# A one-core hybrid decoder step: the order of the down projection and of the rows going back in the later pairs' steps

## Chip, cores and metric

The kernel runs on one core of one Trainium2 chip. The metric is device time of one execution in microseconds (us), lower is better.

## What is computed

The reference is one inference step of two layers over 256 prompt tokens and 32 sample tokens (288 rows of 1024 values, float32). Each layer mixes the tokens (a recurrent group, a convolution group and a retention group) and then applies a mixture of 32 experts of which each token uses two. The change lies in the expert part:

```
def hier_moe(x, wg, bg, we, be, w1, w3, w2):
    ...
    def expert(acc, params):
        w1e, w3e, w2e, ge = params
        h = jax.nn.silu(xt @ w1e) * (xt @ w3e)
        return acc + ge[:, None] * (h @ w2e).astype(jnp.float32), None
```

w1 and w3 of an expert are 1024 x 256, w2 is 256 x 1024, each 1 MB in float32. The two layers hold 192 MB of them, and all of it is read in every execution.

## The kernel before

**Pairs and steps.** The experts are taken in 16 pairs per layer. An expert has 64 slots for tokens, so a pair fills 128 partitions. TensorE (PE) works through `experts2_back(p)`, one call per pair p from 4 to 15 (the first four pairs have a shorter form, `experts2`). In a step of pair p, TensorE issues in this order:

- `up` (L1149) of the pair's first expert: 16 matmuls with w1 and w3, "first up" below;
- `give_back(p - 2, (2, 3))` and `give_back(p - 2, (4,))` (L1195, L1201, L1186), where pair p - 2 is one of `BY_MATMUL`: a 0/1 matrix takes the weighted rows of that pair back to the tokens' places, in three bf16 parts that add up to the float32 value (`y_top`, `y_mid`, `y_low`). Parts 2 and 3 are the second 128 tokens, part 4 the 32 sample rows;
- `down` (L1172) of pair p - 1: the second projection, 8 matmuls with w2, into two PSUM banks (`y0`, `y1`);
- `turn_h` (L749): two transposes of the first expert's hidden values;
- `tokens` half 0 (L749), the second `up`, `tokens` half 1, the second `turn_h`;
- `give_back(p - 1, (0, 1))`: the first 128 tokens of pair p - 1.

`BY_MATMUL` is every pair but 0 to 3, 8 and 9, whose rows go by way of DRAM instead. So parts 2, 3 and 4 are given back in steps 6 to 9 and 12 to 15, in eight steps of a layer. Steps 4, 5, 10 and 11 go through the same function without them. Step 15 has no `tokens`, and its second `turn_h` comes after the function.

**Other engines.** ScalarE (`one_back`, L2235) copies the first hidden values out of PSUM (L2241), waits for part 4 of pair p - 2, whose parts still read the buffer `ysb`, and then writes the two halves of pair p - 1 there (`results`, L2214). Behind them in its order stands the tanh of the first expert (L2233). VectorE (`experts2_back`, L1962) adds parts 2 and 3 (L1950) and 4 (L1954) to `x`, then computes the rest of the first half (L1915), the first expert's hidden product (L1903, L1905), the rest of the second half (L1915), the two low parts (L1921), and takes the next pair's tokens out of PSUM (L1895). `give_back(p - 1, (0, 1))` waits for the low parts (L1199). In steps 13 to 15 VectorE also adds rows that were read back from DRAM (L1938).

**Weights.** SyncE issues all weight loads on one queue, in a fixed order (L669 to L693), into a ring of 12 places of 1 MB. In its step p it issues w1 and w3 of the first expert of p, then waits for `y1` of pair p - 3 and issues the w2 of pair p - 1 (L557, `expert2`), then w1 and w3 of the second expert. `up` and `down` wait for the landings (`granule`). GpSimd gathers the token rows and builds the 0/1 matrices (L2376).

Of the kernel before, what the change touches and what calls it, by code (L numbers as in the profile page):

```python
# [205 lines left out]
def build(nc, ins, outs):  # L206
# [11 lines left out]
    with ExitStack() as ctx:  # L218
# [151 lines left out]
        def weight13(e, j, k):  # L370

            if (e, j) == (THIRD, 0):
                return third_w1[k]
            if e == EARLY:
                k0, a = [pc for pc in (early_w1, early_w3)[j] if pc[0] <= k][-1]
                return a[:, FE * (k - k0):FE * (k - k0) + FE]
            if e == SPARE:
                return (spare_w1, spare_w3)[j][:, k, :]
            return ring[:, 3 * (e % 4) + j, FE * k:FE * k + FE]

        def weight2(e, f, j):

            if e == EARLY:
                f0, j0, a = [pc for pc in early_w2 if pc[0:2] <= (f, j)][-1]
                return a[:, 512 * (j - j0):512 * (j - j0) + 512]
            if e == SPARE:
                return spare_w2[f][:, 512 * j:512 * j + 512]
            return ring[:, 3 * (e % 4) + 2, 1024 * f + 512 * j:1024 * f + 512 * j + 512]
# [103 lines left out]
        def xfreed(eng, kind, u, it, l):  # L492
            b, n = expert_job(kind, u, it, l)
            eng.wait_ge(bank_free[b], n + 1)

        def pair_of(p):

            return p % 2, p // 2

        def granule(eng, l, g, use):  # L500

            spared = [e // 4 for e in (EARLY, SPARE, *((THIRD,) if g % 3 == 0 else ())) if e % 4 == g // 3]
            per = 1 + (g >= 8) + GROUPS - len(spared)
            k = {"in": 0, "out": 1}[use] if isinstance(use, str) else 1 + (g >= 8) + use[0] - sum(it < use[0] for it in spared)
            eng.wait_ge(granule_in[g], 16 * (l * per + k + 1))
# [231 lines left out]
        def _(pe):  # L737
# [10 lines left out]
            def transpose(out, in_, n):  # L748
                return pe.transpose(out, in_, ident[0:n, 0:n])  # L749
# [42 lines left out]
            for l in range(DEPTH):  # L792
# [319 lines left out]
                def begin(kind, u, it):  # L1112
                    b, n = expert_job(kind, u, it, l)
                    pe.wait_ge(bank_free[b], n)
                    return psum[:, b, :]

                def finish(i, kind, u, it=0):
                    i.then_inc(bank_full[expert_job(kind, u, it, l)[0]], 1)

                def tokens(g2, it, halves=(0, 1)):  # L1120

                    par = g2 % 2
                    if 0 in halves:
                        pe.wait_ge(gath[par], 16 * (l * GROUPS + it + g2 // 2 + 1))
                    for kind, k0 in [(("x0", 0), ("x1", 4))[h] for h in halves]:
                        b = begin(kind, g2, it).rearrange("p (k s) -> p k s", k=4)
                        r = rows[:, par, :].rearrange("p (m k) -> p m k", k=KT)
                        for k in range(4):
                            i = transpose(b[:, k, :], r[:, :, k0 + k], 128)
                        finish(i, kind, g2)  # L1130

                def up(u, it):

                    e = 4 * it + u
                    if e in (EARLY, SPARE, THIRD):
                        pe.wait_ge(spare13_in, 16 * 15 * (l + 1))
                    if e not in (EARLY, SPARE):
                        if e != THIRD:
                            granule(pe, l, 3 * u, (it,))
                        granule(pe, l, 3 * u + 1, (it,))  # L1140
                    if u % 2 == 0:
                        xfreed(pe, "x0", u // 2, it, l)
                    b = begin("h", u, it)
                    s = slice(SLOTS * (u % 2), SLOTS * (u % 2) + SLOTS)
                    for k in range(KT):
                        if (u % 2, k) == (0, 4):
                            xfreed(pe, "x1", u // 2, it, l)
                        for j in range(2):
                            i = pe.matmul(b[64 * j:64 * j + 64, 0:FE], xsT[:, u // 2, k, s], weight13(e, j, k), start=k == 0,  # L1149
                                          stop=k == KT - 1, skip_group_check=True)  # L1150
                    finish(i, "h", u)

                def turn_h(u, it):
                    xfreed(pe, "h", u, it, l)
                    b = begin("hT", u, it)
                    for f in range(2):
                        i = transpose(b[:, 128 * f:128 * f + 128], hsb[:, u % 2, 128 * f:128 * f + 128], 128)
                    finish(i, "hT", u)

                def down(pair, it):  # L1160

                    for u in (2 * pair, 2 * pair + 1):
                        if 4 * it + u in (EARLY, SPARE):
                            pe.wait_ge(spare2_in, 16 * 5 * (l + 1))
                        else:
                            granule(pe, l, 3 * u + 2, (it,))
                    xfreed(pe, "hT", 2 * pair + 1, it, l)
                    for j in range(2):
                        b = begin(f"y{j}", pair, it)
                        for f in range(2):  # L1170
                            for q in range(2):
                                i = pe.matmul(b[64 * q:64 * q + 64, :], hT[:, q, f, :], weight2(4 * it + 2 * pair + q, f, j), start=f == 0,  # L1172
                                              stop=f == 1, skip_group_check=True)
                        finish(i, f"y{j}", pair)

                def give_back(p, parts):

                    pair, it = pair_of(p)
                    turn_ = l * len(BY_MATMUL) + BY_MATMUL.index(p)
                    if 0 in parts:  # L1180
                        pe.wait_ge(back_ready, turn_ + 1)
                    if 4 in parts:
                        b = begin("back4", pair, it)
                        for n_, y in enumerate((y_top, y_mid, y_low)):
                            for q in range(4):
                                i = pe.matmul(b[32 * q:32 * q + 32, 0:256], back[:, pair, SEQ:NT], y[:, 256 * q:256 * q + 256],  # L1186
                                              start=n_ == 0, stop=n_ == 2, skip_group_check=True)
                        finish(i, "back4", pair, it)
                        return
                    banks = []  # L1190
                    for a in parts:
                        if a < 2:
                            xfreed(pe, f"y{a % 2}", pair, it, l)
                        banks.append(begin(f"back{a}", pair, it))
                        pe.matmul(banks[-1], back[:, pair, 64 * (a - a % 2):64 * (a - a % 2) + 128], y_top[:, 512 * (a % 2):512 * (a % 2) + 512],  # L1195
                                  start=True, stop=False)
                    for a, b in zip(parts, banks):
                        if a < 2:
                            pe.wait_ge(low_ready, 2 * (turn_ - l) + a + 1)  # L1199
                        for y in (y_mid, y_low):  # L1200
                            i = pe.matmul(b, back[:, pair, 64 * (a - a % 2):64 * (a - a % 2) + 128], y[:, 512 * (a % 2):512 * (a % 2) + 512],  # L1201
                                          start=False, stop=y is y_low)
                        finish(i, f"back{a}", pair, it)
# [25 lines left out]
                def experts2_back(p):  # L1229

                    pair, it = pair_of(p)
                    up(2 * pair, it)
                    if p - 2 in BY_MATMUL:
                        give_back(p - 2, (2, 3))
                        give_back(p - 2, (4,))
                    down(1 - pair, it if pair else it - 1)
                    turn_h(2 * pair, it)
                    if p + 1 < NPAIR:
                        tokens(pair + 1, it, (0,))
                    up(2 * pair + 1, it)  # L1240
                    if p + 1 < NPAIR:
                        tokens(pair + 1, it, (1,))
                        turn_h(2 * pair + 1, it)
                    if p - 1 in BY_MATMUL:
                        give_back(p - 1, (0, 1))
# [1203 lines left out]
```

## Time and profile before

| what | value |
|---|---|
| runs without a profile | 838.98, 837.44, 840.12 us, median 838.98 |
| the profiled execution's own time | 839.37 us |
| its span, first to last instruction | 837.5 us |
| TensorE busy with matmuls | 811.5 us, 97% |
| VectorE, ScalarE, GpSimd busy | 477.8, 176.0, 132.6 us |
| packets of SyncE's queue | 247.01 MB, 77.1% of 16 DMA engines' span |
| granted TensorE clock, mean | 0.996 |

The times are microseconds from the span's start. A row of the trace's timeline gives start, duration, engine, line and operation; rows of one kind that follow each other are merged. A float32 matmul is recorded twice (as two passes), so `x32` in such a row is 16 matmuls of the program. Each matmul's duration includes its passage through the array, so the time of a block is read from its start to the start of the next block. "Issue" as the cause of a wait means that the profile shows no instruction that released it; a landing of a load on which TensorE waited is of that kind here.

### The profile page before, as it was taken

Reading aid. Unit: us, or ns where it says so; the run is one execution under the profiler, and the core shown is the slowest. Engines: PE = TensorE matmul, PEld = TensorE weight load, DVE = VectorE, ACT = ScalarE, POOL = GpSimd, SP = SyncE. Lnnn points to the kernel's source line nnn. Section 1 sums busy time; section 2 is a strip of 40 time slices with the busy share of each in tenths; the row PEclk is TensorE's granted clock in tenths of the full one; section 3 lists DMA queues with packets and bytes.
Section 4 is the critical chain, followed back from the end, with each engine's and each line's share of the span. In section 5 each row is a group of like instructions: output and inputs, shape, how many; then the busy total and the mean of one; then the engine's idle time right before and its main releaser. Section 6 shows DMA issues by size and latency. Waiting matters only on the chain.

```text
span 837.5 us, 13390 instructions
## 1 busy us (share of the span) xinstructions
PE 811.5 (97%) x5250; PEld 459.4 (55%) x5250; DVE 477.8 (57%) x1101; ACT 176.0 (21%) x361; POOL 132.6 (16%) x201
## 2 busy tenths in 40 slices
PE   7999999999999999999999999999999999999995
PEld 4664554586555545455466545547755545555452
DVE  3497788264115554467655977764611455446676
ACT  3214122311221111211221221142022111121113
POOL 0031020011121202431000400200211311115120
PEclk9999999999999999999999999999999999999999
DMA  9942973879999999999990329348799999999971
GB/s 321 321 148 122 374 186 99 290 251 393 415 416 414 414 416 413 413 400 414 348 349 6 151 107 295 106 104 332 303 406 414 417 412 418 413 414 392 414 318 61
DMA packets 91962, 259.64 MB, mean 310 GB/s; under 512 B 30764, under 2 KB 42432, under 8 KB 76218
## 3 DMA queue, kind: packets, MB, share of 16 engines
q1 hardware_dynamic: 82426, 247.01, 77.1%
q0 software_dynamic: 7680, 8.91, 3.2%
q10 hardware_dynamic: 1792, 2.84, 0.9%
q8 instruction: 44, 0.72, 0.4%
q14 instruction: 20, 0.16, 0.1%
HBM read 265.22 MB, written 15.18 MB: 335 GB/s over the span
## 4 chain that ended last, share of the span: by engine, by line
PE 89%; DVE 5%; issue 2%; SPq 2%; ACT 1%; DMA 1%; DVEq 0%; ACTq 0%
PE psum L1149 28%; PE psum L1172 13%; PE psum L809 13%; PE psum L749 8%; PE psum L818 7%; PE psum L1006 4%; PE psum L1201 4%; PE psum L1195 2%; PE psum L828 2%; PE psum L755 1%; PE psum L1045 1%; DMA ring<-in_w_in 1%; PE psum L1186 1%; PE psum L884 1%; PE psum L1035 1%
## 5 line engine op out<-in xcount | busy, mean ns | idle before, releaser
L1149 PE MATMUL psum<-ring,arena 128*64 128x256 f32 x1888 | 220.5, 382 | 2.7 <-issue 1.2
L1149 PEld LDWEIGHTS psum<-ring,arena 128*64 128x64 f32 x1888 | 135.5, 137 | 70.5 <-issue 12.1
L1172 PE MATMUL psum<-ring,arena 128*64 128x512 f32 x480 | 116.2, 596 | 1.7 <-issue 1.7
L809 PE MATMUL psum<-ring,uT 128*128 128x512 f32 x256 | 113.6, 596 | 0.9 <-DVE uT L1383 0.9
L1950 DVE TENSOR_TENSOR x<-x,psum 128x512 f32<-128x512 f32 x80 | 51.4, 683 | 50.3 <-PE psum L1201 45.2
L1895 DVE TENSOR_TENSOR arena<-psum,gff 128x512 f32<-128x512 f32 x64 | 43.6, 686 | 61.0 <-PE psum L749 61.0
L809 PEld LDWEIGHTS psum<-ring,uT 128*128 128x128 f32 x256 | 47.6, 190 | 55.2 <-issue 54.2
L2353 POOL DMA_INDIRECT rows<-xn_scratch,sg x32 | 33.7, 1054 | 233.7 <-PE psum L749 118.1
L2214 ACT ACTIVATE arena<-psum,sg 128x512 f32<-128x512 f32 x64 | 44.0, 687 | 114.9 <-PE psum L1172 113.0
L1903 DVE SCALAR_TENSOR_TENSOR arena<-arena,psum 128x128 f32<-128x128 f32 x64 | 18.4, 287 | 85.7 <-ACT arena L2233 72.1
L1172 PEld LDWEIGHTS psum<-ring,arena 128*64 128x64 f32 x480 | 35.4, 137 | 54.6 <-issue 52.8
L818 PE MATMUL psum<-uT,ring 128*128 128x288 f32 x256 | 63.8, 407 | 0.7 <-DMA ring<-in_w_in 0.7
L1006 PE MATMUL psum<-ring,mixT 128*128 128x512 f32 x128 | 58.9, 612 | 0.0
L2241 ACT ACTIVATE arena<-psum 128x256 f32<-128x256 f32 x48 | 18.4, 383 | 186.1 <-PE psum L1149 186.1
L1470 DVE SCALAR_TENSOR_TENSOR cb<-glp,prm,cb 128x256 f32<-128x256 f32 x120 | 55.8, 534 | 0.6 <-DVE hst L1622 0.4
L818 PEld LDWEIGHTS psum<-uT,ring 128*128 128x128 f32 x256 | 48.1, 190 | 14.6 <-DMA ring<-in_w_in 1.1
L749 PE MATMUL psum<-const,rows 128*128 128x128 f32 (+1 forms) x304 | 47.9, 286 | 0.0
L749 PEld LDWEIGHTS psum<-const,rows 128*128 128x128 f32 (+1 forms) x304 | 39.1, 192 | 13.8 <-issue 12.8
L1915 DVE TENSOR_TENSOR v<-arena 128x512 f32<-128x512 f32 x36 | 24.8, 688 | 32.6 <-ACT arena L2214 32.6
L1006 PEld LDWEIGHTS psum<-ring,mixT 128*128 128x128 f32 x128 | 24.3, 195 | 28.1 <-issue 27.7
L2376 POOL TENSOR_SCALAR kT<-const,sg 128x128 bf16<-128x128 f32 (+3 forms) x60 | 36.7, 626 | 18.0 <-PE psum L1186 17.4
L1954 DVE TENSOR_TENSOR x<-x,psum 32x256 f32<-32x256 f32 x80 | 33.0, 413 | 0.8
(350 smaller groups left out, 908.9 us busy)
## 6 DMA issues: line engine op xcount, KB each, us to landing
ring<-in_moe_w SPq DMA_DIRECT2D x178, 1024.0 KB, 18.0
ring<-in_w_in SPq DMA_DIRECT2D x24, 1024.0 KB, 13.8
ring<-in_w_out SPq DMA_DIRECT2D x8, 1024.0 KB, 7.3
y_scratch<-in_w_out SPq DMA_DIRECT2D x1, 2304.0 KB, 17.8
arena<-in_state_ret SPq DMA_DIRECT2D x16, 128.0 KB, 5.9
out<-arena SPq DMA_DIRECT2D x16, 128.0 KB, 2.5
xn_scratch<-rows ACTq DMA_DIRECT2D x4, 512.0 KB, 4.5
mixT<-in_moe_w SPq DMA_DIRECT2D x2, 1024.0 KB, 4.9
```

The lines of the kernel that those rows point to most:

```text
L749: return pe.transpose(out, in_, ident[0:n, 0:n])
L809: i = pe.matmul(b, uTk[:, k, 128 * t:128 * t + 128], w[:, k, :], start=k == 0, stop=k == KT - 1)
L818: i = pe.matmul(b, w[:, k, 128 * (c % 4):128 * (c % 4) + 128], uTk[:, k, :], start=k == 0, stop=k == KT - 1)
L1006: i = pe.matmul(b, mixT[:, k, 128 * t:128 * t + 128], w[:, :, k, :], start=k == 0, stop=k == 3, skip_group_check=True)
L1149: i = pe.matmul(b[64 * j:64 * j + 64, 0:FE], xsT[:, u // 2, k, s], weight13(e, j, k), start=k == 0, stop=k == KT - 1, skip_group_check=True)
L1172: i = pe.matmul(b[64 * q:64 * q + 64, :], hT[:, q, f, :], weight2(4 * it + 2 * pair + q, f, j), start=f == 0, stop=f == 1, skip_group_chec ...
L1470: chain[c] = own(STT(dst, glp[:, c, k:k + SEQ], w, dst, ALU.mult, ALU.add))
L1895: T(xsT[:, g2 % 2, k0:k0 + 4, :], psum[:, b, :].rearrange("p (k s) -> p k s", k=4), g3[:, k0:k0 + 4, :], ALU.mult).then_inc(bank_free[b], 1)
L1950: i = T(s, s, psum[:, b, :], ALU.add)
L2214: A(ysb[:, 512 * j:512 * j + 512], psum[:, b, :], ACT.Copy, scale=gate_col[:, pair:pair + 1]).then_inc(bank_free[b], 1)
L2353: pool.indirect_dma_start(out=rows[:, g % 2, :], out_offset=None, in_=xn_dram, in_offset=bass.IndirectOffsetOnAxis(ap=gidx[:, g:g + 1], ax ...
L2376: i = pool.tensor_scalar(back[:, g % 2, o:o + n] if g < NPAIR - 1 else back_last[:, o:o + n], C("iota")[:, 0:n], tok[:, t, g:g + 1], None, ...
```

## The change

```diff
@@ -1230,11 +1230,11 @@ (experts2_back, on TensorE)
                     pair, it = pair_of(p)
                     up(2 * pair, it)
+                    down(1 - pair, it if pair else it - 1)
+                    turn_h(2 * pair, it)
                     if p - 2 in BY_MATMUL:
                         give_back(p - 2, (2, 3))
                         give_back(p - 2, (4,))
-                    down(1 - pair, it if pair else it - 1)
-                    turn_h(2 * pair, it)
                     if p + 1 < NPAIR:
                         tokens(pair + 1, it, (0,))
                     up(2 * pair + 1, it)
```

`down` of pair p - 1 and the first `turn_h` are issued right behind the first `up`, and parts 2, 3 and 4 of pair p - 2 behind them. The instructions are the same ones. The orders on VectorE, ScalarE, GpSimd and SyncE are unchanged.

TensorE in step 6 of the first layer, before: first up, parts 2 and 3 (L1195, L1201), part 4 (L1186), down (L1172), the transposes of the hidden values (`arena`) and those of the next tokens (`rows`).

```order
L1149 MATMUL psum<-ring,arena 64x256 x16
L1195 MATMUL psum<-arena,kT 128x512 x2
L1201 MATMUL psum<-v,kT 128x512
L1201 MATMUL psum<-kT 128x512
...
L1186 MATMUL psum<-arena,kT 32x256 x4
L1186 MATMUL psum<-v,kT 32x256 x4
L1186 MATMUL psum<-kT 32x256 x4
L1172 MATMUL psum<-ring,arena 64x512 x8
L749 MATMUL psum<-const,arena 128x128 x2
L749 MATMUL psum<-const,rows 128x128 x4
```

The same place after the change:

```order
L1149 MATMUL psum<-ring,arena 64x256 x16
L1172 MATMUL psum<-ring,arena 64x512 x8
L749 MATMUL psum<-const,arena 128x128 x2
L1195 MATMUL psum<-arena,kT 128x512 x2
L1201 MATMUL psum<-v,kT 128x512
...
L1186 MATMUL psum<-arena,kT 32x256 x4
L1186 MATMUL psum<-v,kT 32x256 x4
L1186 MATMUL psum<-kT 32x256 x4
L749 MATMUL psum<-const,rows 128x128 x4
```

Down and the hidden transposes have gone ahead of the nine rows that give rows back (two L1201 rows are left out each time).

TensorE in step 15, where no tokens follow, after the change: part 4 of pair 13, the second up, and then the first two parts of pair 14.

```order
L1186 MATMUL psum<-arena,kT 32x256 x4
L1186 MATMUL psum<-v,kT 32x256 x4
L1186 MATMUL psum<-kT 32x256 x4
L1149 MATMUL psum<-ring,arena 64x256 x16
L1195 MATMUL psum<-arena,kT 128x512 x2
L1201 MATMUL psum<-v,kT 128x512
```

Before, down and the transposes stood between part 4 and the second up; now only the second up stands between part 4 and the next give_back.

## Rows read from the trace of the kernel before

**Rows 1.** The page, DMA throughput in 40 slices of the span.
```profile
GB/s 321 321 148 122 374 186 99 290 251 393 415 416 414 414 416 413 413 400 414 348 349 6 151 107 295 106 104 332 303 406 414 417 412 418 413 414 392 414 318 61
```
**Rows 2.** TensorE's waits: line, released by, total us, times, longest us.
```profile
PE psum L1172 <- issue: 1.7, 2, 0.9
PE psum L910 <- DVE S L1699: 1.4, 2, 0.7
```
**Rows 3.** Timeline of TensorE, step 6 of layer 0: start, us, operation.
```profile
258.38 3.67 PE L1149 MATMUL psum<-ring,arena 128*64 128x256 f32 x32
261.99 0.63 PE L1195 MATMUL psum<-arena,kT 128*128 128x512 bf16 x2
262.46 0.39 PE L1201 MATMUL psum<-v,kT 128*128 128x512 bf16 x1
...
263.88 3.65 PE L1172 MATMUL psum<-ring,arena 128*64 128x512 f32 x16
267.47 0.44 PE L749 MATMUL psum<-const,arena 128*128 128x128 f32 x2
267.74 0.61 PE L749 MATMUL psum<-const,rows 128*128 128x128 f32 x4
268.28 0.65 PE L1149 MATMUL psum<-ring,arena 128*64 128x256 f32 x4
```
**Rows 4.** The same view, step 10 of layer 0, nothing given back.
```profile
320.04 3.67 PE L1149 MATMUL psum<-ring,arena 128*64 128x256 f32 x32
323.55 3.60 PE L1172 MATMUL psum<-ring,arena 128*64 128x512 f32 x16
327.08 0.44 PE L749 MATMUL psum<-const,arena 128*128 128x128 f32 x2
```
**Rows 5.** The same view, step 13 of layer 0, then of layer 1.
```profile
365.48 0.63 PE L1195 MATMUL psum<-arena,kT 128*128 128x512 bf16 x2
...
368.17 3.65 PE L1172 MATMUL psum<-ring,arena 128*64 128x512 f32 x16 [0.73 <-issue]
...
373.10 3.67 PE L1149 MATMUL psum<-ring,arena 128*64 128x256 f32 x32 [0.47 <-issue]
...
777.71 3.65 PE L1172 MATMUL psum<-ring,arena 128*64 128x512 f32 x16 [0.93 <-issue]
```
**Rows 6.** Three w2 loads by themselves: issue time, time to landing.
```profile
L557 SPq DMA_DIRECT2D ring<-in_moe_w x1: 471/471/471, 327.6 to 327.6; - x1
DMA to landing us min/median/max: 21.2/21.2/21.2
...
L557 SPq DMA_DIRECT2D ring<-in_moe_w x1: 2272/2272/2272, 341.0 to 341.0; - x1
DMA to landing us min/median/max: 27.1/27.1/27.1
...
L557 SPq DMA_DIRECT2D ring<-in_moe_w x1: 3943/3943/3943, 358.1 to 358.1; - x1
DMA to landing us min/median/max: 26.0/26.0/26.0
```
**Rows 7.** Stretches: us, busy by engine, clock, DMA share, GB/s.
```profile
238.00:344.00 106.00, 105.55 (x785) 57.09 (x782) 52.15 (x103) 18.98 (x46) 19.70 (x33) 1.00 1.02 415
141.10:144.40 3.30, 3.30 (x5) 1.35 (x4) 2.37 (x5) 0.00 (x0) 0.00 (x0) 0.50 0.14 30
```
**Rows 8.** Timeline of VectorE, step 6 of layer 0.
```profile
263.10 1.28 DVE L1950 TENSOR_TENSOR x<-x,psum 128x512 f32<-128x512 f32 x2 [3.76 <-PE psum L1201]
264.30 1.69 DVE L1954 TENSOR_TENSOR x<-x,psum 32x256 f32<-32x256 f32 x4
...
268.47 0.29 DVE L1903 SCALAR_TENSOR_TENSOR arena<-arena,psum 128x128 f32<-128x128 f32 x1 [1.04 <-ACT arena L2233]
...
269.60 1.29 DVE L1921 TENSOR_TENSOR kT<-v 128x512 bf16<-128x512 f32 x2
270.81 0.68 DVE L1895 TENSOR_TENSOR arena<-psum,gff 128x512 f32<-128x512 f32 x1
```

## Prediction

> **What bounds the kernel.** I read the page's slices first, then TensorE's waits, then the timeline of whole steps, and last when the weight loads land. The waits say that TensorE hardly waits in the expert steps: 1.7 us at down, in two waits, in both layers together [rows 2]. The timeline of step 6 shows why a move gives little by itself: the blocks stand against each other without a pause, 3.61 us for the first up, 1.89 us for parts 2, 3 and 4, 3.59 us for down, 0.27 us for the two transposes, 0.54 us for the four of the tokens [rows 3]. The slices and the stretch from 238 to 344 us say that the DMA engines are just as full: 415 GB/s at a share of 1.02, flat from one slice to the next [rows 1, 7]. So two things run side by side at nearly the same pace, TensorE and the weight stream, and the reader should look for where they touch. They touch in step 13: down waits 0.73 us in layer 0 and 0.93 us in layer 1 for "issue", which is the landing of w2, and the second up of layer 0 waits 0.47 us [rows 5]. The w2 load issued at 341.0 us takes 27.1 us, so it lands at 368.1 us, and down starts at 368.17 [rows 5, 6].
>
> **Part 1: the move in a step in which nothing is late.** The work is the same. What differs is what stands beside what. In step 10 down follows up directly, and up lasts 3.51 us and down 3.53 us, against 3.61 and 3.59 in step 6 [rows 3, 4]. That is about 0.15 us less in a step. The new neighbours (part 4, then the tokens' transposes) have no row; the nearest is part 4 before down, whose length I keep, so this term lies between 0 and 0.15 us a step, and I take 0.15. The Trainium skill, "TensorEngine Tiling (Array Packing)", Key Properties, says that changing the tiling mode drains TensorE. The change removes one of five changes of mode in a step, and this trace agrees in sign, by that 0.15 us. By the rule alone all 16 steps would gain, 2.4 us in all. But whatever steps 6 to 12 gain ends at the wait of step 13, which goes by the landing.
>
> **Part 2: down comes 1.89 us sooner, w2 does not.** SyncE's queue is full throughout, so an earlier issue only queues longer; the order of loads is unchanged, and w2 of pair 12 is issued after the down of step 11, which isn't touched. I therefore leave every landing where it is. Down of step 13 starts at 368.17 us as before, but TensorE arrives there 1.89 us sooner plus the 0.73 us that it waited already, plus 0.75 us gained in steps 6 to 9 and 12 (part 1), so it pauses about 3.4 us, and 3.7 us in layer 1. Behind the down now stand 1.89 us of parts 2 to 4 that used to be done ahead of it. This is the term that costs. Layer 0: from down at 368.17, the rest of the step is 3.53 + 0.27 + 1.89 + 0.53 + 3.60 + 0.55 + 0.27 + 1.43 = 12.07 us, so step 14 begins at 380.24 instead of 379.12. Up takes 3.51 to 383.75; w2 of pair 13, issued at 358.1, lands at 384.1 [rows 6], so down starts at 384.2. Another 12.07 leads to 396.3, and the second up of step 15 begins at 396.3 + 3.51 + 3.53 + 0.27 + 1.89 = 405.5 us against 404.5 before: **+1.0 us**. Of the 1.89, 0.47 and two smaller waits are absorbed, and 0.15 to 0.25 a step is gained. Layer 1 the same way from 777.71 gives 814.6 against 813.55: **+1.0 us**. The bounds for a layer are 0 (all absorbed) and 1.9 (nothing is). The other steps have margin. The closest is step 12: w2 of pair 11, issued at 327.6, takes 21.2 us and lands at 348.8 [rows 6], and down, now at 351.6 by the step's own rhythm, moves to about 349.0. I cost these steps at nothing: what is lost there is time that step 13 would wait anyway.
>
> **Part 3: ScalarE and VectorE.** ScalarE may write pair p - 1 only once part 4 of pair p - 2 has been made, and that is now the last thing rather than the first. Count from t, the start of parts 2 and 3. VectorE adds parts 2 and 3 at t + 1.11 and part 4 at t + 2.31 for 1.69 us [rows 3, 8]. The results of pair p - 1 are written from t + 2.0 to t + 3.3, so VectorE finds them ready at t + 4.0 and runs on without pause: rest 0.6, the hidden product at t + 4.6, the low parts 1.13 later, done at t + 6.4 and t + 7.0, and the next tokens from t + 6.9 to t + 7.6 (the distances are those of [rows 8]). TensorE wants the low parts at t + 6.84 + 0.46 = t + 7.3, and the tokens at t + 8.27. So the chain fits, by 0.6 us or more, in every step but 15: **0 us**. If the cover is gone, each tenth beyond costs 1.4 us over 14 steps. In step 15 the two token blocks are missing: the give_back of pair 14 begins at t + 1.89 + 3.60 = t + 5.5, wants the first low part 0.46 us later (the distance of the first two rows of give_back in [rows 3]), at t + 5.95, and gets it at t + 6.45; the second follows 0.15 us late. That is **+0.65 us** a layer, 1.3 in all, between 0 and 1.5 with my readings wrong by 0.2 either way. GpSimd gets its gate 1.1 us later; its matrices are needed a step later, so 0.
>
> **Part 4: the clock in the new pause.** TensorE has no pause over 1 us in the expert steps today. One fall of the clock is in the trace: 0.50 granted from 141.1 to 144.4 us [rows 7], that is 1.2 instead of 2.4 GHz, right after a stretch with a wait of 0.7 us and small matmuls [rows 2]. A pause of 3.4 to 3.7 us is a longer lull than that. If the clock falls, up to 3.3 us of work run at half speed: 1.7 us lost at most, 0 if it doesn't fall or is low only during the pause; layer 0 hides 0.4 of it in the wait of step 14. I take the middle, **0.85 us a layer, 1.7 in all**, since the nearest row shows a fall after less. The Trainium skill, "TensorE: Matmul & The Clock Gate", Loop structure matters more than you think, names a wait for a DMA inside the loop as what lets the clock fall. By it both pauses end at the low clock, and at the full price the sum would be 6.3 us instead of 5.0; the wait of 0.93 us in layer 1 [rows 5] shows no fall, so this trace doesn't decide it.
>
> **Sum.** 1.0 + 1.0 + 1.3 + 1.7 = +5.0 us on the profiled execution's 839.37 us, so 844.4; the median of the runs is 838.98, 0.4 lower, and I put the forecast on it: **844.0 us**. A change of 0.3%, 2.5 us, is about what a measurement can tell here.
>
> **Rivals.** (1) *No fall of the clock*: the same waits without part 4, +3.3 us, 842.3. For it: the pause is short; against: the row at 141 us. (2) *The landings move with the issue, or the wait in step 13 is another's*: then no pause appears, and all 16 steps give their 0.15 us: 1.3 - 2.4 = -1.1, 837.9. It is the case on the other side, not slower: its place is down of step 13, its price the 0.15 us a step, and it decides if w2 lands 3 us sooner than now. Against it stands a queue at a share of 1.02. If in addition the low parts are in time in step 15, the time is 836.6. (3) *VectorE's chain is longer than I count*, because TensorE's part 4 or the results take longer: with 0.9 us more it runs past the next up's start by 0.3 us in 14 steps, +4.2 on top, 848.2. The margin of 0.6 us speaks against it. (4) *Only step 13 matters*: the low parts in step 15 are early enough, +2.0 to +3.7.
>
> **Chances.** Forecast with the clock falling in one or both layers 0.50; rival 1 0.22; rival 2 0.10 (of it 0.04 at 836.5 or below); rival 3 0.08; rival 4 0.10. The range 840.5 to 846.5 holds the forecast, rival 1 and nearly all of rival 4; it leaves out rivals 2 and 3. Faster by over 0.3%: 0.04. Within 0.3% (836.5 to 841.5): 0.06 of rival 2, half of rival 4 and a little of rival 1, 0.18. Slower: 0.78.
>
> **What would show it.** In the profile after: TensorE's wait at L1172 for "issue" grows from 1.7 us to about 7, nearly all in step 13 of both layers, with down of step 13 at the same time from the layer's start; no new wait at L1149 for VectorE's tokens (L1895) in steps 6 to 14; a wait of about 0.65 us at L1201 in step 15 released by L1921; a granted clock of 0.5 for up to 3.3 us from the end of the pause; up and down in the changed steps 3.51 and 3.53 us. A down of step 13 that starts 2 us sooner would refute part 2; waits on L1895 in all steps would refute part 3.

## The result, and the profile after

The changed kernel takes 844.90 us (median of 20 runs, 839.47 to 849.38) against 838.93 of the kernel before (20 runs, 836.51 to 841.76): a ratio of 1.0064, 95% interval 1.0051 to 1.0077, so 5.4 us slower (4.3 to 6.5). The forecast was +5.0 us, 844.0. The same kernel run again on another occasion (experiment 8) gave 1.0082 (1.0060 to 1.0104).

The profiled execution after took 841.89 us with a span of 840.1, one of its faster ones, and shows where the time goes. TensorE's waits of the kernel after (line, released by, total us, times, longest), to be set against [rows 2]:

```profile
PE psum L1172 <- issue: 4.9, 2, 2.8
...
PE psum L910 <- DVE S L1699: 1.4, 2, 0.7
...
PE psum L1201 <- DVE kT L1921: 0.9, 2, 0.5
```

Down waits 4.9 us instead of 1.7, still in two waits, and there are two new waits of 0.5 us for the low parts (`y_mid` and `y_low`, made by VectorE at L1921). Nothing new stands at L1149, where a late chain on VectorE would show. TensorE's timeline in step 13 of layer 0, and then the down of layer 1, against [rows 5]:

```profile
359.72 3.67 PE L1149 MATMUL psum<-ring,arena 128*64 128x256 f32 x32
366.16 3.65 PE L1172 MATMUL psum<-ring,arena 128*64 128x512 f32 x16 [2.77 <-issue]
369.74 0.44 PE L749 MATMUL psum<-const,arena 128*128 128x128 f32 x2
370.24 0.39 PE L1195 MATMUL psum<-arena,kT 128*128 128x512 bf16 x1
...
371.44 0.30 PE L1186 MATMUL psum<-arena,kT 128*32 128x256 bf16 x4
...
371.90 0.71 PE L749 MATMUL psum<-const,rows 128*128 128x128 f32 x4
372.54 0.65 PE L1149 MATMUL psum<-ring,arena 128*64 128x256 f32 x4
...
778.15 0.65 PE L1172 MATMUL psum<-ring,arena 128*64 128x512 f32 x2 [2.12 <-issue]
```

The first up is followed by a pause of 2.8 us, then down, and the parts that used to fill this time stand behind it. The load that down waited for, by itself (L557 of the kernel after), and the stream around it:

```profile
L557 SPq DMA_DIRECT2D ring<-in_moe_w x1: 2275/2275/2275, 338.7 to 338.7; - x1
...
DMA to landing us min/median/max: 27.3/27.3/27.3
```
```profile
238.00:344.00 106.00, 105.43 (x778) 57.83 (x786) 52.90 (x107) 18.72 (x46) 20.45 (x34) 1.00 1.02 415
```

It was issued at 338.7, 27.3 us before it landed at 366.0, with 27.1 before [rows 6], and the DMA engines moved the same 415 GB/s at a share of 1.02 as in [rows 7]. The issue of this load hangs on the down of step 11, which isn't moved. The load that does follow a moved down, that of step 12, is w2 of pair 13. The load of its first expert in layer 0, after and then before:

```profile
L557 SPq DMA_DIRECT2D ring<-in_moe_w x1: 4558/4558/4558, 351.2 to 351.2; - x1
...
DMA to landing us min/median/max: 28.0/28.0/28.0
```
```profile
L557 SPq DMA_DIRECT2D ring<-in_moe_w x1: 2762/2762/2762, 355.3 to 355.3; - x1
...
DMA to landing us min/median/max: 26.3/26.3/26.3
```

Counted from the start of step 6 (256.48 and 258.38) it is issued 2.2 us sooner, takes 1.7 us longer and lands 0.5 us sooner. An earlier down brings the weights hardly sooner.

Step 6, where w2 is in time, against [rows 3]:

```profile
256.48 3.67 PE L1149 MATMUL psum<-ring,arena 128*64 128x256 f32 x32
259.98 3.60 PE L1172 MATMUL psum<-ring,arena 128*64 128x512 f32 x16
263.51 0.44 PE L749 MATMUL psum<-const,arena 128*128 128x128 f32 x2
264.01 0.39 PE L1195 MATMUL psum<-arena,kT 128*128 128x512 bf16 x1
...
265.67 0.72 PE L749 MATMUL psum<-const,rows 128*128 128x128 f32 x4
266.32 0.87 PE L1149 MATMUL psum<-ring,arena 128*64 128x256 f32 x6
```

The first up takes 3.50 us and down 3.53, as in [rows 4]. But the tokens' transposes behind part 4 take 0.65 us to the next up instead of 0.54. From the first up to the second the step now takes 9.84 us where it took 9.90.

VectorE in step 6 of the kernel after, against [rows 8], and TensorE in step 15:

```profile
264.88 1.28 DVE L1950 TENSOR_TENSOR x<-x,psum 128x512 f32<-128x512 f32 x2 [7.45 <-PE psum L1201]
266.08 1.69 DVE L1954 TENSOR_TENSOR x<-x,psum 32x256 f32<-32x256 f32 x4
267.70 0.68 DVE L1915 TENSOR_TENSOR v<-arena 128x512 f32<-128x512 f32 x1
268.41 0.29 DVE L1903 SCALAR_TENSOR_TENSOR arena<-arena,psum 128x128 f32<-128x128 f32 x1
...
269.54 1.28 DVE L1921 TENSOR_TENSOR kT<-v 128x512 bf16<-128x512 f32 x2
270.74 1.28 DVE L1895 TENSOR_TENSOR arena<-psum,gff 128x512 f32<-128x512 f32 x2
```
```profile
403.29 3.67 PE L1149 MATMUL psum<-ring,arena 128*64 128x256 f32 x32
407.14 0.39 PE L1195 MATMUL psum<-arena,kT 128*128 128x512 bf16 x1 [0.17 <-issue]
407.97 0.40 PE L1201 MATMUL psum<-v,kT 128*128 128x512 bf16 x1 [0.45 <-DVE kT L1921]
```

VectorE now works from part 2 to the tokens without a pause. In step 6 the first half of the tokens is out at about 271.4 and the next up starts at 272.17, so it fits. In step 15 the low parts come 0.45 us too late.

The two traces can also be compared from the first up of step 6 on, which leaves out what differs in the mixing part. To the second up of step 15 it is 146.8 us instead of 146.1 in layer 0 and 146.2 instead of 145.8 in layer 1; to the start of the layer's last down it is 155.0 instead of 153.6 and 154.4 instead of 153.3. That makes +1.5 and +1.1 us in an execution in which the clock did not fall in the expert steps, where the forecast without the clock had +1.65 each.

### The profile page after: what moved, and what is told of

The parts are those of the page before. It is cut to its first block, busy times and chain, and to the rows that moved or that the text cites. A ratio compares the mean times of both kernels' runs of the same rounds, so it can differ in the third digit from the quotient of the medians.

```text
span 840.1 us, 13356 instructions
## 1 busy us (share of the span) xinstructions
PE 809.3 (96%) x5216; PEld 459.6 (55%) x5250; DVE 474.6 (56%) x1101; ACT 174.4 (21%) x361; POOL 127.3 (15%) x201
## 4 chain that ended last, share of the span: by engine, by line
PE 87%; DVE 6%; issue 2%; SPq 2%; DMA 1%; ACT 1%; DVEq 0%; POOLq 0%; ACTq 0%
PE psum L1149 27%; PE psum L1172 13%; PE psum L809 12%; PE psum L749 9%; PE psum L818 7%; PE psum L1006 4%; PE psum L1201 4%; PE psum L828 2%; PE psum L1195 1%; PE psum L1045 1%; DMA ring<-in_w_in 1%; PE psum L1186 1%; PE psum L884 1%; PE psum L1035 1%; SPq L540 1%
## 5 line engine op out<-in xcount | busy, mean ns | idle before, releaser
L1149 PE MATMUL psum<-ring,arena 128*64 128x256 f32 x1888 | 220.4, 382 | 1.2 <-DVE arena L1895 1.2
L1149 PEld LDWEIGHTS psum<-ring,arena 128*64 128x64 f32 x1888 | 133.2, 137 | 71.1 <-issue 10.1
L1172 PE MATMUL psum<-ring,arena 128*64 128x512 f32 x480 | 115.5, 593 | 4.9 <-issue 4.9
L2214 ACT ACTIVATE arena<-psum,sg 128x512 f32<-128x512 f32 x64 | 42.2, 685 | 131.3 <-PE psum L1186 88.7
L1172 PEld LDWEIGHTS psum<-ring,arena 128*64 128x64 f32 x480 | 36.6, 137 | 57.2 <-issue 53.8
L749 PE MATMUL psum<-const,rows 128*128 128x128 f32 (+1 forms) x304 | 50.1, 294 | 0.1
L2376 POOL TENSOR_SCALAR kT<-const,sg 128x128 bf16<-128x128 f32 (+3 forms) x60 | 32.3, 553 | 25.2 <-PE psum L1186 24.6
```

Source lines behind the costliest of these rows:

```text
L2214: A(ysb[:, 512 * j:512 * j + 512], psum[:, b, :], ACT.Copy, scale=gate_col[:, pair:pair + 1]).then_inc(bank_free[b], 1)
```

## Experiments

All times are medians. The product of the time and one minus the mean granted clock is what the low clock (1.2 instead of 2.4 GHz) can have taken in an execution. In the profiled executions 1.8 to 3.3 us of it lie behind the last matmul and cost nothing, and the product does not say in which part of the kernel the rest lies. "Rest" is the mean time less that product. The kernel before ran beside the experiments on three occasions, with mean products of 4.4 us (experiments 1 to 4), 4.6 us (5 to 8) and 3.6 us (9 to 11).

| kernel | us | ratio to before, 95% | mean product, us | rest, us |
|---|---|---|---|---|
| before, 78 runs beside the experiments | 838.8 to 839.2 | | 4.2 | 834.9 |
| changed, 26 runs | 844.90, 844.84 | 1.0064 (1.0051 to 1.0077) | 6.4 | 838.5 |
| 1: eight small matmuls in the pause | 843.68 | 1.0062 (1.0039 to 1.0086) | 5.1 | 838.2 |
| 2: new order in step 13 alone | 843.59 | 1.0054 (1.0025 to 1.0083) | 5.9 | 837.3 |
| 3: all but step 13 | 842.33 | 1.0045 (1.0027 to 1.0064) | 4.9 | 837.1 |
| 4: step 15 alone | 840.84 | 1.0020 (1.0001 to 1.0039) | 4.7 | 836.1 |
| 5: old order, less w2 loaded | 835.97 | 0.9970 (0.9954 to 0.9986) | 4.9 | 831.2 |
| 6: new order, less w2 loaded | 836.51 | 0.9977 (0.9964 to 0.9990) | 5.2 | 831.6 |
| 7: steps 6 to 9 and 12 alone | 839.28 | 1.0004 (0.9988 to 1.0019) | 4.1 | 834.7 |
| 9: six small matmuls in the pause | 843.36 | 1.0050 (1.0028 to 1.0073) | 5.2 | 838.2 |
| 10: all but step 15 | 844.24 | 1.0061 (1.0037 to 1.0085) | 6.4 | 838.3 |
| 11: step 14 alone | 840.23 | 1.0015 (0.9993 to 1.0038) | 4.5 | 836.2 |

One thing in these kernels differs that was not meant to. In experiments 1, 3, 9 and 10 step 13 begins 0.6 to 0.7 us later in both layers: from the second up of step 12 to the first up of step 13 it is 6.4 to 6.6 us, and 5.86 in before, after and all other runs. In step 12, the results on ScalarE and the add on VectorE start 1.4 to 1.6 us after the end of part 4. VectorE's add of part 4 in step 12 in the kernel after, then the last matmuls of part 4, that add, and TensorE's next up in experiment 10 (VectorE's lines are four further on):

```profile
353.63 1.69 DVE L1954 TENSOR_TENSOR x<-x,psum 32x256 f32<-32x256 f32 x4
```
```profile
355.21 0.28 PE L1186 MATMUL psum<-kT 128*32 128x256 bf16 x4
...
356.90 1.70 DVE L1958 TENSOR_TENSOR x<-x,psum 32x256 f32<-32x256 f32 x4 [0.98 <-PE psum L1186]
...
362.51 3.67 PE L1149 MATMUL psum<-ring,arena 128*64 128x256 f32 x32 [0.19 <-DVE arena L1899]
```

In the kernel after the last matmuls of part 4 start at 353.00, and the add follows without a wait. Why the four kernels are late there isn't shown. It comes just ahead of the wait for w2 in step 13 and mostly shortens that wait, so the times say little of it.

**Experiments 5 and 6: is it the stream?** Both orders with fewer bytes on the queue ahead of step 13 (experiment 5 edits the kernel before, experiment 6 the changed one).

```diff
             def expert2(l, it, u):
                 e = 4 * it + u
+                n = 128 if it in (4, 5) else D
-                sp.dma_start(ring[:, 3 * u + 2, :].rearrange("p (f d) -> p f d", f=2),
-                             w2[l, e].rearrange("(f p) d -> p f d", p=128)).then_inc(granule_in[3 * u + 2], 16)
+                sp.dma_start(ring[:, 3 * u + 2, :].rearrange("p (f d) -> p f d", f=2)[:, :, 0:n],
+                             w2[l, e].rearrange("(f p) d -> p f d", p=128)[:, :, 0:n]).then_inc(granule_in[3 * u + 2], 16)
```

> The kernel before, but of w2 of the experts 17 to 23 only the first 128 of 1024 columns are loaded (the rest of each place keeps an older expert's values, so these pairs' outputs are not the reference's): 6.4 MB less on the queue in each layer, some 15 us of the stream, ahead of step 13. Every matmul is still done. Theory A (w2 of step 13 and w3 behind it land late): the waits of 0.7 to 0.9 us at L1172 and about 0.4 us at L1149 in steps 13 to 15 go, 836 to 838 us. Theory B (the waits are not the stream's): as before, 838.8.

> The changed kernel with the same short loads. Theory A (the cost of the new order is the late w2 in step 13, what stands behind it, the falls of the clock there, and the low parts in step 15): against the kernel with short loads and the old order it keeps only the low parts, 0.5 us a layer, less 0.25 us a layer in step 15 and 0.06 us in each other step: -0.5 to +0.5 us instead of +6; no wait at L1172 over 0.3 us, granted clock as in the old order. Theory C (the chain from ScalarE to VectorE costs something in every step, or the new order itself makes the clock fall): +2 us or more stays.

Measured: 835.97 and 836.51 us, the first just below the expected 836 to 838. The new order costs 0.5 us, at the upper edge of the expected band, instead of the 5.6 us that the medians of the same occasion give without the short loads, and neither kernel waits at down any more. TensorE's timeline in step 13 of the new order with short loads (its lines are one further on, L1173 is down):

```profile
361.22 3.67 PE L1150 MATMUL psum<-ring,arena 128*64 128x256 f32 x32
364.73 3.60 PE L1173 MATMUL psum<-ring,arena 128*64 128x512 f32 x16
...
368.76 0.39 PE L1196 MATMUL psum<-arena,kT 128*128 128x512 bf16 x1
```

What is left of TensorE's waits in the same kernel's expert steps:

```profile
PE psum L1202 <- DVE kT L1922: 0.9, 2, 0.4
```

The waits for the low parts stay. In the two traces a layer from the first up of step 6 to its last down is 0.2 us longer with the new order: the low parts cost 0.8 us, the steps gain 0.6. That is 0.4 of the half us. The mean products, 4.9 and 5.2 us, are as near as their scatter: without the pause a lower clock of the new order isn't seen. Theory A holds, and theory C, a cost in every step, falls.

**Experiments 2, 7, 3 and 11: which step?** The order was chosen by step (against the kernel before):

```diff
                     up(2 * pair, it)
+                    if p in NEW:
+                        down(1 - pair, it if pair else it - 1)
+                        turn_h(2 * pair, it)
                     if p - 2 in BY_MATMUL:
                         give_back(p - 2, (2, 3))
                         give_back(p - 2, (4,))
-                    down(1 - pair, it if pair else it - 1)
-                    turn_h(2 * pair, it)
+                    if p not in NEW:
+                        down(1 - pair, it if pair else it - 1)
+                        turn_h(2 * pair, it)
```

Here `NEW` stands for (13,), then (6, 7, 8, 9, 12), then all eight but 13, then (14,).

> The kernel before with the new order in step 13 alone. Theory A (the pause in step 13 is the whole cost but for the low parts in step 15, worth 0.5 us a layer): +3.5 to +5.5 us, 842.5 to 844.5, with clock falls as in the changed kernel. Theory C (the cost is spread over all eight steps, each with a little wait on the chain from ScalarE to VectorE): one eighth, below +1 us.

> The kernel before with the new order in steps 6 to 9 and 12 alone. Theory A: these steps have w2 in time, gain 0.06 us each and lose it at the wait of step 13: 838.3 to 839.5 us, no difference that can be measured. Theory C: five eighths of the cost, about +3.5 us.

> The changed kernel with the old order in step 13 alone. Theory A: 1.0 us for the low parts in step 15 stay, 0.06 us a step is gained and lost again at the wait in step 13, which grows to about 1.1 us a layer, and the new order in step 14 can wait some tenths for w2: 838.9 to 840.5 us. Theory C: seven eighths of the cost stay, 843 to 844.5 us.

> The kernel before with the new order in step 14 alone. I expected no cost from step 14 when step 13 keeps the old order, and the third experiment read +3.5 us with a wait of 1.4 us for w2 in step 14. Theory A (whichever late step comes first takes the wait for w2): +1 to +2.5 us, a wait of about 1.4 us at L1172 in step 14 of layer 0, less in layer 1. Otherwise 838.5 to 839.5 us.

Step 13 alone costs 4.8 us of medians, as much as the whole change within the intervals. The five earlier steps cost nothing. So far theory A. But the change without step 13 read +3.5 us, above what I expected; and the wait that I expected at its down of step 13 isn't there. TensorE's waits of that kernel (all but step 13), and its down in step 14 of layer 0:

```profile
PE psum L1172 <- issue: 1.9, 2, 1.4
PE psum L1149 <- issue: 1.9, 5, 0.6
```
```profile
376.45 3.67 PE L1149 MATMUL psum<-ring,arena 128*64 128x256 f32 x32 [0.61 <-issue]
381.54 1.04 PE L1172 MATMUL psum<-ring,arena 128*64 128x512 f32 x3 [1.42 <-issue]
```

I had read the margin of step 14 from the changed kernel, where step 13 has already pushed everything back. When step 13 keeps the old order, down of step 14 comes ahead of its own w2, and waits there. Step 14 alone shows nearly the same wait, 1.3 us, and its rest is 0.8 us above that of the kernel before beside it; its ratio, 1.0015, is not clear of 1. By the medians the single steps don't add up (13 alone +4.8, 14 alone +1.4, 15 alone +2.0, all together +5.4 to +6). Their intervals alone would leave room for it, but the traces show why they shouldn't add: in the changed kernel, with its long wait in step 13, down of steps 14 and 15 doesn't wait for w2. They draw on one stream's lateness.

**Experiments 4 and 10: the low parts in step 15.** `NEW` is (15,), then all but 15.

> The kernel before with the new order in step 15 alone. Theory A (TensorE waits there for the low parts, 0.5 us a layer, and part 4 then meets the second up directly, which takes 0.25 less): +0.5 to +1.2 us, 839.4 to 840.1, with two waits of about 0.5 us at L1201 for L1921. If the low parts are hidden: 838.4 to 838.9.

> The changed kernel with the old order in step 15 alone. Theory A: the wait for the low parts goes (1.0 us in both layers), the second up gets back the 0.25 us a layer that it saved: 843.5 to 844.5 us, and no wait for L1921. If step 15 costs as much inside the change as it did alone (+1.8 us): 843.0.

Alone, step 15 read +2.0 us by the medians, above the expected 0.5 to 1.2; the ratio makes it +1.7, with an interval from 0.1 to 3.3. The profile shows the two waits for the low parts (L1925 in this kernel, four lines further on). Waits of TensorE with the new order in step 15 alone, and its down in step 15 of layer 0:

```profile
PE psum L1149 <- issue: 1.4, 3, 0.5
...
PE psum L1172 <- issue: 1.0, 2, 0.6
PE psum L1201 <- DVE kT L1925: 0.9, 2, 0.5
```
```profile
398.16 1.90 PE L1172 MATMUL psum<-ring,arena 128*64 128x512 f32 x7 [0.57 <-issue]
```

This down of step 15 waits 0.57 us for its w2, as that of step 14 did in experiment 11: a cost that I had left out. Without step 15 the change reads 844.24, in the expected band, and the low parts hold nobody up. The difference of 0.7 us to the changed kernel is inside the scatter; the size of this term comes from the trace, not from the times.

**Experiments 1, 9 and 8: the clock.** Small matmuls in the pause, into the bank that down then overwrites (against the changed kernel):

```diff
                     up(2 * pair, it)
+                    if p in (13,):
+                        keep_clock(begin("y0", 1 - pair, it if pair else it - 1), 8)
                     down(1 - pair, it if pair else it - 1)
```

Experiment 9 has 6 for 8; experiment 8 is the changed kernel again.

> The changed kernel with eight small matmuls of the identity into the bank of the down projection, issued in step 13 between the first up and down; they fill about 2.1 us of the pause for w2 (2.8 us in layer 0, 2.1 us in layer 1 of the profiled execution) and change no result. Theory A (the pause costs its waiting time, and on top the clock falls to 1.2 GHz in or behind it in many executions, some 1.7 us each): the waiting stays, the falls go; 840.5 to 842.5 us, 2 to 4 below the changed kernel, with the scatter between executions down from 10 us to about 4, and granted clocks of 0.995 and above. Theory B (the scatter and the excess come from the weight stream, the clock is only an effect): as the changed kernel, 844 to 845, clocks down to 0.99 or less.

> As the first experiment, with six small matmuls (1.6 us) in the pause of step 13 instead of eight (2.1 us), so that they end ahead of w2 in both layers. Theory A: the time less the part lost to the half clock stays at 838.3 us as in the changed kernel (eight left 838.2), and what the half clock takes falls from 6.2 to 7.0 us to about 5: 842.5 to 843.8 us. Theory B (the clock has nothing to do with the pause): 844.8 with 6 us or more at the half clock.

> The changed kernel once more, beside the three others on one chip: 844 to 845.5 us, mean granted clock about 0.9925 against 0.995 before. If it were a matter of the chip, the ratio would differ from 1.0064 by more than its interval.

The profile of experiment 8 caught a fall of the clock in the pause. Stretches of that execution (us, busy by engine, granted clock, DMA share, GB/s), and TensorE's timeline of step 13:

```profile
364.00:370.60 6.60, 3.85 (x31) 2.00 (x29) 2.83 (x3) 0.38 (x1) 0.65 (x2) 1.00 1.03 417
370.60:374.00 3.40, 3.40 (x11) 1.14 (x8) 0.00 (x0) 0.00 (x0) 0.00 (x0) 0.50 1.00 411
```
```profile
369.24 5.35 PE L1172 MATMUL psum<-ring,arena 128*64 128x512 f32 x16 [2.75 <-issue]
374.53 0.44 PE L749 MATMUL psum<-const,arena 128*128 128x128 f32 x2
```

After a pause of 2.75 us the clock stood at 0.50, 1.2 GHz, from 370.6 to 374.0, and down took 5.29 us to its successor instead of 3.58: one fall, 1.7 us. In layer 1 of the same execution a pause of 3.2 us passed without a fall, and the execution profiled first had none in either pause. Nor had the profiled execution of experiment 2, with pauses of 2.6 and 3.6 us in step 13 (its stretches from the start of each pause):

```profile
365.50:375.00 9.50, 6.79 (x45) 3.10 (x46) 2.01 (x5) 1.36 (x3) 0.00 (x0) 1.00 1.03 417
777.70:788.00 10.30, 6.63 (x43) 3.00 (x46) 1.80 (x5) 1.22 (x3) 0.00 (x0) 1.00 1.02 414
```

Nor had that of experiment 10, with 2.5 and 1.5 us. So of eight unfilled pauses in four profiled executions one had a fall. All 16 other falls that the 13 profiled executions show ahead of their last matmul lie outside the expert steps, in kernels with and without the pause. The slow executions are those with the low clock (849.38 and 849.35 us at mean clocks of 0.991 and 0.987, the fastest, 839.47, at 0.997), so much of the scatter of 10 us is the clock's; how much of it is the pause's isn't shown.

Filled with small matmuls, the pause leaves the rest where it was (838.2 twice, 838.5 without them) and takes the mean product from 6.4 to 5.1 and 5.2, against 4.2 before. Against the kernel before on the same occasion the product is 1.5, 2.4 and 2.8 us higher with the pause unfilled (experiments 2, 8 and 10) and 0.7 and 1.6 us higher with it filled (1 and 9). That is the direction and about half the size that theory A asks for. The medians, 843.68 and 843.36, fall by 1.2 to 1.5 us, the first 1.2 us above what I had expected, the second within it; the scatter is 5.5 us with eight but 7.4 with six, so the claim on the scatter isn't borne out. With six, the profile still has a wait of 1.0 us behind the filling, and whether that keeps the last falls alive is open. Not one of these intervals excludes the changed kernel's ratio. That the pause can cost a fall is shown once, by the trace of experiment 8; that it costs as much as the products rise is argued from the clocks of all runs, and the one fall in eight pauses would make it less.

## Why the prediction was right

**What bounds the kernel.** That TensorE and the weight stream run at nearly one pace and touch in step 13 was right, and experiments 5 and 6 show it: take the lateness of the stream away, and the cost of the order goes from 5.6 us to 0.5.

**Part 1.** Up and down became as short as the rows of step 10 had them, 3.51 and 3.53 us. The kept length of the new neighbours was the error: the tokens' transposes behind part 4 take 0.11 us more. The step gains 0.06 us, not 0.15. The rule of the Trainium skill, "TensorEngine Tiling (Array Packing)", Key Properties, that a change of mode drains TensorE has the sign right and counts one change fewer; in this trace most of what is saved at one place came back behind part 4. As forecast, none of it reached the time (experiment 7, ratio 1.0004).

**Part 2.** Forecast: pauses of 3.4 and 3.7 us at down (its own terms, 1.89 + 0.93 + 0.75, make 3.6 of the second) and +1.0 us a layer. Measured in the two profiled executions: waits of 2.8 and 2.1 us, and 2.75 and 3.2 us. They are shorter than forecast mainly because steps 6 to 12 gained 0.25 us where 0.75 was taken, and in one case because w2 landed early: from the first up of step 6 to the down of step 13 it was 109.8 and 110.0 us before and 109.0 to 110.1 in these two executions (110.8 in one layer of experiment 2, with the pause of 3.6 us). So the landing did not follow the issue, but it moves by up to 1.8 us by itself. To the second up of step 15 the layers took 0.7, 0.3 and 1.4 us longer than before, and 0.7 in the one with the fall once its 1.7 us are taken off, where 1.0 was forecast. Together with part 3 it was to make 3.3 us without the clock; the rest rose by 3.6 us.

**Part 3.** In the changed kernel the chain on VectorE fits in all steps but 15, with 0.7 us to spare where I had reckoned 0.6, and rival 3 is out. Its mechanism does exist: in step 12 of experiments 1, 3, 9 and 10 part 4 is passed on over 1 us late, and TensorE then waits for VectorE. In step 15 the wait for the first low part is 0.45 us. From the second up to the layer's last down the changed kernel takes 8.23 us instead of 7.44 in layer 0, so the low parts cost 0.8 us a layer where 0.65 was forecast.

**Part 4.** Forecast 1.7 us, with a fall priced at 1.7 us and taken half a time in each layer; the mean product rose by 2.2 us, of which it isn't known how much lies in the pause. The Trainium skill, "TensorE: Matmul & The Clock Gate", Loop structure matters more than you think, names a wait for a DMA as what lets the clock fall. This case's traces agree in one pause (2.75 us) and not in seven others (1.5 to 3.6 us), so the full price would have been too much. By the traces alone, one fall in four executions, the term would be 0.4 us and the forecast's half too much as well; four executions are few. The row that the forecast leaned on doesn't decide it either: in the kernel after, the same wait of 0.7 us in the mixing part is followed by a full clock over the same stretch as in [rows 7].

```profile
141.10:144.40 3.30, 3.30 (x12) 1.27 (x14) 2.70 (x6) 0.00 (x0) 0.00 (x0) 1.00 0.09 21
```

**The rivals.** Rival 1, no fall of the clock, gave +3.3 us, 842.3; the interval of the measured difference, 4.3 to 6.5 us, leaves it out, though in the expert steps the first profiled execution shows +2.6 us, and that of experiment 8 +3.6 us without its fall. Rival 2 is refuted by the pause itself, by the landing of w2 and by the flat stream. Rival 4 is refuted as far as the two waits at L1201 go. The forecast was 5.0 us and 5.4 were measured. The mechanism of parts 2 and 3 is shown. That the sum came so near is in part luck: the cost of the pause was taken a little too large (1.0 us a layer against 0.8 in the mean of the four) and that of the low parts too small, which nearly cancel, and the third of the sum that stands for the clock is a middle that no run confirms.

## What to carry to other kernels

Before a consumer of loaded data is moved ahead of other work, look at when its data lands, not at when its inputs from other engines are ready: with a full queue the landing stays nearly where it is (0.5 us sooner here for an issue 2.2 us sooner), and the work that it jumped was what filled the wait. Look in the steps in which the slack is smallest, since an average or a typical step shows none of it, and don't add single steps up. And a new pause on TensorE can cost more than its length, since the clock may fall behind it, as it did in one of eight pauses here.

## What was not expected of the hardware

The clock fell to 1.2 GHz after a pause of only 2.75 us, began to be low 1.4 us after work had started again, and stayed so for 3.4 us of full work; a pause of 3.2 us in the same execution and one of 3.6 us in experiment 2 had no such effect. Such falls also come in the mixing part in some executions and not in others, in the kernel before (at 141 us) and after (at 552 us), which can make up part of the 5 us between the fastest and the slowest run of the kernel before. The weight load that was issued 2.2 us sooner, counted from step 6, landed only 0.5 us sooner, and its issue alone kept SyncE for 4.6 us instead of 2.8. And four matmuls of the transposes behind the 32-column part take 0.11 us longer than behind 128-column work, which no row of before showed.
